# Moving small steps of two transformer layers past each other: one PSUM buffer, index products, gate halves, cross values

## The reference, cut to what matters

```python
for l in range(2):
    xn = rmsnorm(x, norm_mix[l])
    qa, ka, va, qb, kb, vb, qc, kc, vc, qi, ki, wi, gates = split(xn @ w_in[l])
    o_a = chunk_band_attention(qa, ka, va, rel_bias[l])             # units A, 0 to 7
    o_b = subnorm(diff_attention(rope(qb), rope(kb), vb, lam))      # units B, 8 to 15
    # o_c: each query sees the 64 keys with the largest
    # score[q, s] = sum_h relu(rope(qi)[q, h] . rope(ki)[s] / 8) * wi[q, h]
    o_c = dsa_attention(rope(qc), rope(kc), vc, qi, ki, wi, 64)     # units C, 16 to 23
    g = sigmoid(gates)                                              # 6 pieces of 4 chunks
    x = x + (g0 * (o_a @ up_a) + g1 * (o_b @ up_b) + g2 * (o_c @ up_c)) @ w_out[l]
    x = x + cross_attention(rmsnorm(x), mem_n, w_q_x, w_kv_x, w_o_x)  # units X, 24 to 27
    x = x + swiglu(rmsnorm(x), w_gu, w_down)
```

## Time and profile before

| | |
|---|---|
| median of 3 runs | 1813.42 us |
| the runs | 1817.58, 1812.99, 1813.42 us |
| profiled execution | 1817.64 us, of it 1815.6 span |
| mean granted TensorE clock | 0.956 |
| layer 0, layer 1 | from about 683 and 1216 us |
| TensorE, DVE, ACT, GpSimd busy | 91%, 48%, 33%, 3% |

### The profile page before, as it was taken

How to read it: one execution, slowest core, us unless ns; L and a number is a source line. 1 busy time by engine, 2 the same in 40 slices (tenths; PEclk the granted TensorE clock), 3 DMA queues, 4 the chain that set the end, 5 groups by cost and what they waited for, 6 DMA issues and landing times.

```text
span 1815.6 us, 24529 instructions
## 1 busy us (share of the span) xinstructions
PE 1645.6 (91%) x10516; PEld 1315.3 (72%) x10516; DVE 875.9 (48%) x1236; ACT 593.9 (33%) x921; POOL 58.5 (3%) x28
## 2 busy tenths in 40 slices
PE   6967699999999998988899899999989899989997
PEld 5846543444434448878778789999978778879997
DVE  1783311110111018658754476646556755466654
ACT  1030211111011115443441364435344451354442
POOL 0000000000000000015000000000006000000000
PEclk8988699999999999999999999999999999989998
DMA  9052099999999994622424345475532623445550
GB/s 354 1 231 81 25 428 428 429 428 428 428 428 429 428 398 167 227 101 96 160 93 162 116 141 188 162 251 191 186 114 95 207 94 112 153 153 171 169 195 24
DMA packets 123659, 393.70 MB, mean 217 GB/s; under 512 B 4144, under 2 KB 55728, under 8 KB 111280
## 3 DMA queue, kind: packets, MB, share of 16 engines
q1 hardware_dynamic: 123568, 392.38, 56.9%
HBM read 386.34 MB, written 1.05 MB: 213 GB/s over the span
## 4 chain that ended last, share of the span: by engine, by line
PE 67%; DVE 14%; DMA 11%; ACT 5%; issue 2%; SPq 0%; DVEq 0%; ACTq 0%; PEld 0%; PEldq 0%
DMA ring<-w 10%; PE psum L1009 9%; PE psum L789 8%; PE psum L790 8%; PE psum L792 8%; PE psum L1171 5%; PE psum L779 3%; PE psum L1031 3%; DVE outs L1547 3%; PE psum L1234 2%; PE psum L1231 2%; PE psum L1233 2%; ACT probs L1265 2%; DVE w_lo L577 2%; PE psum L820 1%
## 5 line engine op out<-in xcount | busy, mean ns | idle before, releaser
L577 DVE TENSOR_TENSOR w_lo<-raw,w_hi 128x1024 fp32r<-128x1024 f32 x254 | 305.3, 1223 | 195.1 <-ACT w_hi L1268 193.7
L789 PE MATMUL psum<-h_hi,w_hi 128*128 128x256 f32 x1456 | 370.1, 291 | 22.7 <-DVE wi L1861 7.9
L1268 ACT ACTIVATE w_hi<-raw 128x1024 fp32r<-128x1024 f32 x278 | 288.1, 1053 | 281.2 <-PE psum L792 126.3
L790 PE MATMUL psum<-h_hi,w_lo 128*128 128x256 f32 x1456 | 364.1, 287 | 0.0
L789 PEld LDWEIGHTS psum<-h_hi,w_hi 128*128 128x128 f32 x1456 | 284.8, 196 | 29.8 <-issue 12.3
L790 PEld LDWEIGHTS psum<-h_hi,w_lo 128*128 128x128 f32 x1456 | 285.1, 196 | 0.2
L1009 PE MATMUL psum<-ring,outs 128*64 128x512 f32 x1024 | 231.2, 607 | 24.0 <-DMA ring<-w 22.5
L792 PE MATMUL psum<-h_lo,w_hi 128*128 128x256 f32 x1456 | 206.1, 285 | 0.0
L1009 PEld LDWEIGHTS psum<-ring,outs 128*64 128x64 f32 x1024 | 81.3, 140 | 171.7 <-issue 171.7
L1710 DVE TENSOR_TENSOR qk<-big,psum 128x512 f32<-128x512 f32 x16 | 17.3, 1080 | 367.6 <-PE psum L1009 367.6
L792 PEld LDWEIGHTS psum<-h_lo,w_hi 128*128 128x128 f32 x1456 | 189.9, 194 | 0.0
(11 more groups left out here) (257 smaller groups left out, 2127.4 us busy)
## 6 DMA issues: line engine op xcount, KB each, us to landing
...
raw<-w_gu SPq DMA_DIRECT2D x44, 1024.0 KB, 7.7
...
```

The costliest lines, as they stand in the source:

```text
L577: return eng.tensor_tensor(chunk_part(w_lo, n), chunk_raw(n), chunk_part(w_hi, n).bitcast(F32), ALU.subtract)
L789: mm(to, hi[:, k, :], h_hi[:, k, :], start=(k == 0), stop=False)
L790: mm(to, lo[:, k, :], h_hi[:, k, :], start=False, stop=False)
L1268: return nca.activation(out_ap, in_ap, ACT.Copy)
```

## The change

Six edits, in the two layers alone; no arithmetic result is changed.

- `index` is divided: TensorE's and ScalarE's part (`index_product` 0 and 1) stands before apply 7, with other tenants for the buffers; the vector engine's part stays after apply 7.
- `DUO_OF` seats p_vb in duo 3, p_idx in 2, i_0 in 2, i_1 in 0, p_qc in 1, p_kc in 3, p_vc in 0. (Before: 2, 3, 0, 1, 2, 3, 0.)
- Gates 0 and 1 are one tenant of duo 3, gates 2 to 5 another. The vector engine empties a gate piece in two halves of 128 x 512, after parts 1 and 3. TensorE waits before parts 0 and 2 for the half of the piece before; the duo itself is released only after gates 1 and 5.
- `subln` is divided: its sums on TensorE (`subln_sums`) stand before apply 23.
- `cross_v` is divided by token half; the halves stand before scores 25 and scores 26. The keys are copied on a semaphore of their own; apply 24 waits for the values' copy.
- The tree of hT in layer 0 (`mix2`) stands after low 4.

```diff
@@ -156,20 +156,26 @@
     return {s + o: [("gates", piece + i, gate + i, o)] for i, s in enumerate(starts) for o in range(4)}
 
 
+def without_last(steps, step):
+    assert steps[-1] == step
+    return steps[:-1]
+
+
 WORK = ([("norm", "mix"), ("lam",), ("proj", 0, "qa"), ("proj", 1, "ka"), ("proj_v", 2, "va"),
          ("proj", 3, "qb"), ("evac", 0, "qb"), ("proj", 4, "kb"), ("rope", 0, "qb"), ("evac", 1, "kb"),
          ("proj_v", 5, "vb"), ("rope", 1, "kb"), ("index_proj", 6), ("evac", 2, "idx")]
-        + attention(0, 8, {**gate_parts((1, 5), 7, 0), 1: [("index_weights",), ("gates", 7, 0, 0)],
-                           4: [("gates", 7, 0, 3), ("rope", 2, "idx")]})
+        + without_last(attention(0, 8, {**gate_parts((1, 5), 7, 0), 1: [("index_weights",), ("gates", 7, 0, 0)],
+                                        4: [("gates", 7, 0, 3), ("rope", 2, "idx")]}), ("apply", 7))
+        + [("index_product", 0), ("index_product", 1), ("apply", 7)]
         + [("index", 0), ("index", 1), ("proj", 9, "qc"), ("proj", 10, "kc"), ("evac", 3, "qc"), ("evac", 4, "kc"),
            ("proj_v", 11, "vc")]
-        + attention(8, 24, {**gate_parts((9, 13, 17, 21), 12, 2),
-                            10: [("gates", 12, 2, 1), ("rope", 3, "qc")], 11: [("gates", 12, 2, 2), ("rope", 4, "kc")],
-                            25: [("square_b",)]})
-        + [("subln",)] + [("up", 16 + b, b) for b in range(3)]
-        + [("out", 19, 0), ("out", 20, 1), ("norm", "cross"), ("cross_k", 21), ("cross_v", 21), ("sums", "cross"),
+        + without_last(attention(8, 24, {**gate_parts((9, 13, 17, 21), 12, 2),
+                                         10: [("gates", 12, 2, 1), ("rope", 3, "qc")],
+                                         11: [("gates", 12, 2, 2), ("rope", 4, "kc")], 25: [("square_b",)]}), ("apply", 23))
+        + [("subln_sums",), ("apply", 23), ("subln",)] + [("up", 16 + b, b) for b in range(3)]
+        + [("out", 19, 0), ("out", 20, 1), ("norm", "cross"), ("cross_k", 21), ("sums", "cross"),
            ("cross_q", 22)]
-        + attention(24, 28, {}) + [("cross_o", 23), ("norm", "ffn")]
+        + attention(24, 28, {25: [("cross_v", 21, 0)], 26: [("cross_v", 21, 1)]}) + [("cross_o", 23), ("norm", "ffn")]
         + [("gate_up", 24 + i, i) for i in range(KF // 2)] + [("down", k) for k in range(KF)] + [("down_add",)])
 
 
...
-            for _ in range(4):
-                out += [("split", split), ("low", split)]
+            for i in range(4):
+                out += [("split", split), ("low", split)] + ([("tree", "mix2")] if first == "mix" and not i else [])
                 split += 1
...
-        held = w[0] in ("gates", "probs", "turn", "apply", "cross_q", "sums", "evac", "rope") or (w[0] == "scores" and w[1] >= 24)
+        held = w[0] in ("gates", "probs", "turn", "apply", "cross_q", "sums", "evac", "rope", "index_product", "subln_sums") or (w[0] == "scores" and w[1] >= 24)
...
-        if direct_left and w[0] in ("up", "cross_v", "cross_o"):
+        if direct_left and w[0] in ("up", "cross_v", "cross_o") and not (w[0] == "cross_v" and w[2] == 0):
...
-            names += [f"g_{w[2]}"] if w[3] == 0 else []
+            names += [f"g_{w[2]}"] if w[3] == 0 and w[2] in (0, 2) else []
...
@@ -285,6 +291,9 @@
     return names
 
 
+DUO_OF = {"p_vb": 3, "p_idx": 2, "i_0": 2, "i_1": 0, "p_qc": 1, "p_kc": 3, "p_vc": 0}
+
+
 def seat(names, before, at):
 
 
-            d, others = others % DUOS, others + 1
+            d, others = DUO_OF.get(name, others % DUOS), others + 1
         at[name] = (d, before[d])
         before[d] += 1
...
@@ -1092,8 +1101,11 @@
                                       qiT[rows, cc, t * P:(t + 1) * P], qiT[rows, 2, 0:nk], start=True, stop=True)
                         last.then_inc(idx_done, 1)
                     elif kind == "gates":
-                        i, name, o = w[1], f"g_{w[2]}", w[3]
-                        if o == 0:
+                        i, g, o = w[1], w[2], w[3]
+                        name = "g_0" if g < 2 else "g_2"
+                        if o % 2 == 0 and g not in (0, 2):
+                            pe.wait_ge(gate_scaled, (l * 6 + g) * 2 - 1 + o // 2)
+                        elif o == 0:
                             enter(pe, name, l)
                         split_chunk(i, o, duo(name)[:, o * SEQ:(o + 1) * SEQ], l)
                     elif kind == "scores":
@@ -1106,7 +1118,7 @@
                         elif u == 16:
                             pe.wait_ge(rope_ready, l * 5 + 5)
                         elif u == 24:
-                            freed(pe, "xkv", l)
+                            pe.wait_ge(kx_ready, l + 1)
                             freed(pe, "xq", l)
                         enter(pe, f"u_{u}", l)
                         for r in range(2):
@@ -1129,6 +1141,8 @@
                         u = w[1]
                         ukind, cc, qt, nk, _, _ = unit_aps(u)
                         pe.wait_ge(probsT_ready, l * N_UNITS + u + 1)
+                        if u == 24:
+                            freed(pe, "xkv", l)
                         nt = nk // P
                         to = duo(f"u_{u}")
                         if ukind == "B":
...
@@ -1187,14 +1201,17 @@
                         to = view(duo("xkv"), 0, 4, SEQ)
                         for o in range(2):
                             for k in range(KD):
-                                mm(to[:, o, :], wk[:, k, o * P:(o + 1) * P], memT[:, k, :],
-                                   start=(k == 0), stop=(k == KD - 1))
+                                last = mm(to[:, o, :], wk[:, k, o * P:(o + 1) * P], memT[:, k, :],
+                                          start=(k == 0), stop=(k == KD - 1))
+                        last.then_inc(keys_done, 1)
                     elif kind == "cross_v":
-                        for t in range(TT):
-                            for k in range(KD):
-                                last = mm(to[:, 2 + t, :], memT[:, k, t * P:(t + 1) * P], wk[:, k, SEQ:2 * SEQ],
-                                          start=(k == 0), stop=(k == KD - 1))
-                        last.then_inc(direct_done, 1)
+                        t = w[2]
+                        wk = view(raw_of(w[1]), 0, KD, HALF)
+                        for k in range(KD):
+                            last = mm(view(duo("xkv"), 0, 4, SEQ)[:, 2 + t, :], memT[:, k, t * P:(t + 1) * P],
+                                      wk[:, k, SEQ:2 * SEQ], start=(k == 0), stop=(k == KD - 1))
+                        if t == 1:
+                            last.then_inc(direct_done, 1)
                     elif kind == "cross_o":
                         i = w[1]
                         raw_arrived(pe, i, l)
@@ -1427,7 +1444,7 @@
 
                         if w[3] == 3:
                             g = w[2]
-                            act_e.wait_ge(gate_scaled, l * 6 + g + 1)
+                            act_e.wait_ge(gate_scaled, (l * 6 + g) * 2 + 2)
                             part = gates[:, 4 * g:4 * g + 4, :]
                             f(part, part, ACT.Tanh, scale=0.5).then_inc(gates_ready, 1)
                     elif kind == "scores":
...
@@ -1471,9 +1488,11 @@
                             act_e.wait_ge(mixed_ready, l * 2 + half + 1)
                             f(h_hi[:, half * 4:half * 4 + 4, :], hT[:, half * 4:half * 4 + 4, :], ACT.Copy, scale=0.5
                               ).then_inc(h_hi_ready, 1)
-                    elif kind == "cross_v":
+                    elif kind == "cross_k":
+                        act_e.wait_ge(keys_done, l + 1)
+                        copy(kx, view(duo("xkv"), 0, 2, SEQ)).then_inc(kx_ready, 1)
+                    elif kind == "cross_v" and w[2] == 1:
                         product_done(act_e, w[1], l)
-                        copy(kx, view(duo("xkv"), 0, 2, SEQ)).then_inc(kx_ready, 1)
                         copy(vx, view(duo("xkv"), 512, TT, SEQ)).then_inc(free_of("xkv"), 1)
                     elif kind == "gate_up":
                         i = w[2]
@@ -1770,9 +1789,11 @@
                     elif w == ("tree", "mix") and l == 0:
                         v.wait_ge(sq_ready, 5 + 1)
                         link(halved(sq, sums_z))
-                        v.wait_ge(squares_x, 1)
-                        link(halved(hT, sums_x))
-                        v.scalar_tensor_tensor(sums8[:], sums_x, EPS, sums_z, ALU.mult, ALU.add).then_inc(sums8_ready, 1)
+                    elif w == ("tree", "mix2"):
+                        if l == 0:
+                            v.wait_ge(squares_x, 1)
+                            link(halved(hT, sums_x))
+                            v.scalar_tensor_tensor(sums8[:], sums_x, EPS, sums_z, ALU.mult, ALU.add).then_inc(sums8_ready, 1)
                     elif kind == "tree":
                         v.wait_ge(sq_ready, l * 4 + 5 + {"mix": 1, "cross": 3, "ffn": 4}[w[1]])
```

(17 more changed lines are left out.)

14 lines of the change are left out of this document (7 added, 7 removed).

## The result

| kernel | median, us | range | ratio to the kernel before, run beside it | 95% interval | profiled span |
|---|---|---|---|---|---|
| before | 1814.94 | 1812.99 to 1817.58 | | | 1815.6 |
| changed | 1785.89 | 1782.0 to 1788.57 | 0.9837 | 0.9812 to 0.9862 | 1785.4 |
| changed, beside e10 and e11 | 1787.93 | 1787.22 to 1789.41 | 0.9841 | 0.9825 to 0.9858 | 1786.0 |

A forecast was written before the change was run, and what follows sets the result against it. TensorE, busy 91% of the span, was taken to bound the kernel, so gains lie only in its waits and low clock. Terms 5.1 + 9.2 + 1.0 + 8.0 - 2.2 + 9.4 = 30.5 us off 1813.4 gave 1783 us, range 1768 to 1799.

The forecast's parts named there:

- The tree: Layer 0 start: half the first tree behind low 4 starts chunk 4 earlier, at full clock; 5.1 us gained.
- `p_idx`: First attention, both layers: its own PSUM buffer removes gate chunk 0's wait for `wi`; 5.1 us gained a layer.
- Gate halves: Both attentions: removed release waits mostly return through the exp chain; -0.6 us a layer in the first, +1.0 together in the second.
- Index products: Before apply 7: they fill its 2.08 us wait but meet new waits of 1.0 and 0.9; 0.1 us gained a layer.
- Index work: Layer 0: the vector engine's index products start before GpSimd, so the selection ends early; 8.0 us gained.
- the index products fall behind GpSimd: Rival: index work falls behind GpSimd in both layers, its gain drops to 2.5 us, layer 1 pays 8.0; 1796 us, chance 0.13.
- Sub-norm: Sums before apply 23: one wait of about 2.7 us, a new one of 0.4; 2.2 us lost over both layers.
- the slower rival: Rival: the gap before the sub-norm's sums keeps the clock low through the up products; 1866 us, chance 0.03.
- Cross values: Cross attention: value halves between scores fill waits; 4.7 us a layer, 9.4 in all, 5.8 a layer if the clock holds.
- Waits come through whole: Rival: the chain has unseen slack, the halves cost nothing and all TensorE's removed waits are gained; 1763 us, chance 0.09.
- Late gate-and-up weights: Rival: the first gate-and-up weights arrive late, by up to 4 us a layer; 1791 us, chance 0.05.
- Nothing: Rival: the change moves waits without shortening the path, all hidden by the exp chain; 1812 us, chance 0.04.

The follow-up runs named there:

- e10: Changed kernel with the gates' emptying moved behind the apply and the sub-norm's sums put back behind apply 23: 1766.98 us, ratio 0.9723.
- e11: Kernel before, with only the low part of chunk 37 computed by the vector engine instead of GpSimd: 1809.54 us, ratio 0.9964.
- e5: Kernel before, with only the sum tree split so that its first part runs before the last chunk: 1808.67 us, ratio 0.9956.
- e6: Kernel before, with only the index projection and the values swapping their PSUM buffers: 1802.3 us, ratio 0.9914.
- e1: Changed kernel with each gate emptied in one go behind its last product, as before, instead of in two halves: 1789.49 us, ratio 0.9851.
- e2: Changed kernel with the emptying of each gate's first half moved behind the apply on the vector and scalar engines: 1769.98 us, ratio 0.9743.
- e8: Changed kernel with the index products put back behind apply 7: 1786.7 us, ratio 0.9834.
- e12: Kernel of e10 with the low parts of chunks 47 to 50 also given to GpSimd instead of the vector engine: 1763.53 us, ratio 0.9707.
- e3: Changed kernel with the sums of the sub-norm put back behind apply 23: 1780.69 us, ratio 0.9804.
- e4: Changed kernel with the cross attention's values computed in one piece ahead of the token sums, as before: 1789.69 us, ratio 0.9852.

## Where the prediction was right, and where only its sum was

1. **The tree, +5.1.** Right: 5.4 us in the changed kernel, 5.35 alone (e5). Chunk 4 starts 2.8 us earlier, and the full clock came back behind a wait of 1.63 us, as taken.
2. **`p_idx`, +5.1 a layer.** Right in mechanism, and in size for layer 0: 5.3 and 6.3 alone (e6). The chunk behind the wait for `wi` took 5.4 us in layer 1 (1331.19 to 1336.61), at the low clock for longer than the 4.3 us one of layer 0 from which I had priced both. The whole first attention of layer 1 brought 7.4 against 4.6 forecast and an upper end of 5.9: that term was mis-sized, by 2.8 us. The chunk is 1.1 of it. Another 1.2 lie in the index products: from the first of them to the first chunk of qc it is 2.8 us in layer 1 of the kernel before, at the low clock, and 1.6 in layer 0, and in the changed kernel 4.3 in both.
3. **Gate halves, about nothing.** Right in mechanism: 7.2 us of release waits go and the waits for ScalarE's copies grow by as much (e1: 18.0 to 25.1). The size was too low up to the up products: -0.2 forecast, 3.3 us by positions (1.3 in layer 0, 2.0 in layer 1), some 1.5 of it in the sub-norm. Over both layers whole 1.0 us of it is left. What the prediction said of the place of each half, ahead of the next scores' evacuation and therefore in the chain, was the most useful sentence in it. e2 shows it, since moving only the place is worth 16 to 18 us. I had priced this chain as something the change ran into, and not asked for its price over both attentions.
4. **Index products, +0.1.** The two waits worked out as 1.0 and 0.9 measured 1.17 and 0.69, and the whole move is worth next to nothing (e8: 0.4 us a layer by positions).
5. **Index work, +8.0.** The size was right (7.4 us over the stretch), the mechanism was right, and the step from edit to mechanism was wrong in part. The vector engine's sums do wait for GpSimd (e11, whose 8.1 us over the stretch are the term's 8.0). That they escape it does not need the products' new place: e8 keeps the gain without it, and e5 and e6 find 6.8 and 6.5 us in this stretch without any edit of the index work, of which 4.4 and 5.0 are left after what the low clock costs just ahead. Nor does it need a later start of GpSimd: in both, and in layer 1 of the kernel before, GpSimd starts as far ahead of the sums as in layer 0 of the kernel before, but then pauses for 1.0 to 1.25 us. I had read only the three quick sums of layer 1 and not the first one before them, 2.03 us, which meets GpSimd there too. It was a cost of GpSimd's operations following each other without a gap, in layer 0 alone, and my rival "the index products fall behind GpSimd" was the other side of the same coin. Nor did the sums become cheap: those of t=1 grew from 6.2 us to 10.2 in the changed kernel, so that the selection ended 5.5 us before TensorE came to unit 8, the rotation took 4.8 of them, and a wait of 0.23 us for `low 47` shows that nothing was left; I had put the margin at over 10 us. The Trainium skill, "SBUF — State Buffer", section "SBUF: two separate sides", has the rule by which this goes: whoever starts first keeps the shared ports for the whole instruction. The rows of e12 agree within 0.2 us (3.41 us from 844.66; GpSimd ended at 847.00, and 1.22 more is 848.22 against 848.07), and so do those with an input in PSUM, which the rule leaves out.
6. **Sub-norm, -2.2.** The wait came as worked out (2.66 and a new one of 0.48), but the term was mis-sized: against the kernel before it is -2.4 in layer 0 and -1.0 in layer 1, exactly the prediction's lower end, and e3 gives back 2.7 us at the sums and 1.2 in the up products. The prediction priced the low clock over the sums alone; the rows of layer 0 show it at 0.81 over the first 10 us of the up products. This is the mild form of the slower rival: it did reach into the up products, by 1.9 us and not by 30, and only in layer 0. The wait alone does not decide it: behind the same 2.66 us in layer 1 and in e8, and behind 3.20 in e1, the up products have 1.00. What decides it stays open.
7. **Cross values, +9.4.** Mis-sized: 7.3 us in the stretch against the kernel before (2.9 and 4.4), 6.6 by e4. The two waits stand where they were worked out (0.73 for 0.8; 2.16 for 2), scores 27 come 13.0 us behind scores 24 for 12.65, and at scores 27 the gain is 3.9 us in each layer for 4.2. What failed is the 0.5 a layer added for a clock that would hold to the output product. That product takes 8.4 us in layer 0 where it took 7.1 in the kernel before; but e4, with the values back in their old place, has 8.5 there, so this slow one is not the move's doing. By e4 the stretch behind scores 27 costs 0.6 us a layer instead of bringing 0.5.

The rivals. *Waits come through whole* (1763) is refuted by e1. *Index products behind GpSimd in both layers* (1796): they came first in both. *Late gate-and-up weights* (1791): no wait for them. *Nothing* (1812): excluded by the interval.

The sum met the result within 3 us because the first attentions came out 3.4 us high and the stretch from the first up product of layer 0 to layer 1 came out 3.6 low. That is luck of the sum and not proof of its terms.
